# Block 1 of a mixer kernel computes two gates with eight plain products, and the weight sums for the later blocks move there

## The reference

```python
h = rms_norm(x, norm_g[l]) * (1.0 + scale[:, None, :]) + shift[:, None, :]
proj = h @ w_in[l]
...
o_gate = jax.nn.sigmoid(proj[..., OFF_O:OFF_ZM])
z_mlstm = proj[..., OFF_ZM:OFF_G]
...
hm = mlstm_chunkwise(q, k, v, ig, lf)
...
mlstm_out = hm.astype(x.dtype) * o_gate * jax.nn.silu(z_mlstm)
```

## Time and profile before

| | before |
|---|---|
| median of three runs | 1773.0 us |
| the profiled execution | 1772.9 us |
| its span, first to last instruction | 1771.1 us |
| PE busy | 1720.6 us, 97% |
| DVE, ACT, POOL busy | 1261.6, 709.6, 310.4 us |
| mean granted TensorE clock | 0.990 |
| DMA | 387.75 MB, mean 219 GB/s |

### The profile page before, as it was taken

How to read it: one execution, slowest core, us unless ns; L and a number is a source line. 1 busy time by engine, 2 the same in 40 slices (tenths; PEclk the granted TensorE clock), 3 DMA queues, 4 the chain that set the end, 5 groups by cost and what they waited for, 6 DMA issues and landing times.

```text
span 1771.1 us, 25354 instructions
## 1 busy us (share of the span) xinstructions
PE 1720.6 (97%) x8921; PEld 1475.0 (83%) x8921; DVE 1261.6 (71%) x2599; ACT 709.6 (40%) x1636; POOL 310.4 (18%) x265
## 2 busy tenths in 40 slices
PE   5996999999999999999999999999999999999998
PEld 5885787988888888988889888888889888898886
DVE  7784687666876678766876668766787667876683
ACT  4443334343443535334343434345343353433421
POOL 0022113021130302103030121303022030300300
PEclk9998999999999999999999999999999999999999
DMA  9998884679646895569846797468955598466852
GB/s 334 337 319 336 247 247 108 229 218 288 171 156 212 231 297 139 191 191 250 277 104 220 209 277 199 122 237 238 289 140 192 189 259 266 117 216 199 253 167 83
DMA packets 393554, 387.75 MB, mean 219 GB/s; under 512 B 258300, under 2 KB 283860, under 8 KB 392916
## 3 DMA queue, kind: packets, MB, share of 16 engines
q1 hardware_dynamic: 378196, 363.44, 66.9%
q10 hardware_dynamic: 15232, 22.69, 4.2%
HBM read 323.99 MB, written 62.06 MB: 218 GB/s over the span
## 4 chain that ended last, share of the span: by engine, by line
PE 87%; DVE 5%; DMA 4%; issue 2%; ACT 1%; SPq 0%; POOL 0%; ACTq 0%; DVEq 0%; POOLq 0%
PE ps_acc L717 19%; PE ps_acc L719 19%; PE ps_acc L718 19%; PE ps_num L719 4%; PE ps_num L717 4%; PE ps_num L718 4%; PE ps_kv L717 2%; PE ps_kv L718 2%; PE ps_kv L719 2%; PE ps_sco L1007 2%; PE ps_num L1026 1%; PE ps_kv L1032 1%; PE ps_num L1025 1%; DMA s_kept<-sb_x_res 1%; DVE sb_ada_raw L1691 1%
## 5 line engine op out<-in xcount | busy, mean ns | idle before, releaser
L717 PE MATMUL ps_acc<-sb_hT_hi,sb_w_split 128*128 128x512 f32 x1024 | 406.8, 397 | 1.1 <-DVE sb_w_split L1839 1.0
L719 PE MATMUL ps_acc<-sb_hT_hi,sb_w_split 128*128 128x512 f32 x1024 | 400.0, 391 | 0.0
L718 PE MATMUL ps_acc<-sb_hT_lo,sb_w_split 128*128 128x512 f32 x1024 | 399.2, 390 | 0.0
L719 PEld LDWEIGHTS ps_acc<-sb_hT_hi,sb_w_split 128*128 128x128 f32 x1024 | 192.6, 188 | 41.4
L717 PEld LDWEIGHTS ps_acc<-sb_hT_hi,sb_w_split 128*128 128x128 f32 x1024 | 192.9, 188 | 40.9 <-issue 1.9
L718 PEld LDWEIGHTS ps_acc<-sb_hT_lo,sb_w_split 128*128 128x128 f32 x1024 | 193.0, 188 | 37.7
L1544 POOL TENSOR_TENSOR sb_w_split<-sb_w_raw,sb_w_split 128x512 fp32r<-128x512 f32 x84 | 116.5, 1395 | 559.5 <-ACT sb_w_split L1108 559.4
L1108 ACT ACTIVATE sb_w_split<-sb_w_raw 128x512 fp32r<-128x512 f32 x140 | 85.9, 631 | 80.3 <-DMA sb_w_raw<-s_kept 76.5
L2067 DVE SCALAR_TENSOR_TENSOR sb_acc_cv<-sb_shifted,sb_par,sb_acc_cv 128x512 f32<-128x512 f32 x96 | 73.7, 767 | 60.7 <-ACT sb_acc_cv L1377 58.2
L1861 DVE TENSOR_TENSOR sb_w_split<-sb_w_raw,sb_w_split 128x512 fp32r<-128x512 f32 x56 | 56.9, 1017 | 69.3 <-ACT sb_w_split L1108 69.0
L1555 POOL TENSOR_TENSOR sb_h_rs<-sb_h_var,sb_mhalf 128x4 f32<-128x4 f32 x32 | 32.4, 1012 | 400.3 <-DVE sb_h_var L2161 400.3
(11 more groups left out here) (287 smaller groups left out, 3935.0 us busy)
## 6 DMA issues: line engine op xcount, KB each, us to landing
sb_w_split<-w_kept SPq DMA_DIRECT2D x288, 512.0 KB, 4.4
sb_w_split<-w_kept SPq DMA_DIRECT2D x56, 520.0 KB, 4.5
sb_w_raw<-s_kept SPq DMA_DIRECT2D x112, 256.0 KB, 4.3
sb_w_raw<-w_in SPq DMA_DIRECT2D x76, 256.0 KB, 4.6
sb_x_res<-x SPq DMA_DIRECT2D x34, 512.0 KB, 4.7
w_kept<-sb_w_split SPq DMA_DIRECT2D x32, 512.0 KB, 6.2
out<-sb_qT SPq DMA_DIRECT2D x32, 512.0 KB, 2.9
sb_x_in<-x SPq DMA_DIRECT2D x112, 128.0 KB, 3.9
```

The lines of the kernel that those rows point to most:

```text
L717: pe.matmul(dst, st_hi, mv_hi, start=start, stop=False, skip_group_check=resumed)
L718: pe.matmul(dst, st_hi, mv_lo, start=False, stop=False, skip_group_check=resumed)
L719: return pe.matmul(dst, st_lo, mv_hi, start=False, stop=stop, skip_group_check=resumed)
```

## The change

Block 1 does its z and o as block 0 does: eight plain products, two gates of eight k-steps in four chunks, in place of seven products. Each gate has four banks of its own there. Its zo stage has 16 units, eight from `w_kept` and eight raw (w_in's o columns; ACT splits them, POOL makes the low parts), so `UNITS` and `TILE_UNITS` have three kinds of blocks. The weight sums leave block 0. In block 1 they have four buffers, `s_raw`, over the memory of `mixm`, the row broadcasts, `fg`, `x_in` and `x_res`; SP loads them at units 26 to 29, DVE sums all four after `turn_keys`, SP stores them at units 35 to 38 and waits for the stores at unit 40, ahead of the next block's x; ACT waits for them ahead of its row broadcasts. `keep_keys` stands at units 33 to 40, two for each unit.

```diff
-SUM_TILES = {8 + 2 * r: r for r in range(4)}
-SUM_LOADS = {28: 0, 35: 1, 39: 2, 43: 3}
-SUM_STORES = {34 + 4 * r: r for r in range(4)}
+SUM_LOADS = {26: (0,), 27: (1,), 28: (2,), 29: (3,)}
+SUM_STORES = {35: 0, 36: 1, 37: 2, 38: 3}
+SUMS_KEPT = 40
...
+        s_raw = nc.alloc_sbuf_tensor_at("sb_s_raw", [P, 4, 2, D], F32, offset=sums_at)
-        zo_first = [acc[0], acc[1], bro, num[1]]
+        zo_first = [[[acc[0], acc[1], bro, num[1]]] * 2, [[acc[0], acc[1], sco, bro], [num[0], num[1], kv[0], kv[1]]]]
...
             def load_sums(r):
-                if r == 0:
-                    sp.wait_ge(x_T, PREPS)
-                else:
-                    sp.wait_ge(w_sum_kept, 16 * r)
+                sp.wait_ge(acc_full, TASKS)
+                sp.wait_ge(o_ready, NC)
+                sp.wait_ge(x_turned, NC)
...
# first_block, SP
-                    if m in SUM_STORES:
-                        keep_sums(SUM_STORES[m])
-                    if m in SUM_LOADS:
-                        load_sums(SUM_LOADS[m])
...
-                        sp.wait_ge(w_sum_kept, 64)
...
+            def second_block():
+                for m in range(LOW, UNITS[1]):
+                    if QK_END <= m < TILE_UNITS[1]:
+                        load_zo(1, m - QK_END)
+                    else:
+                        load_w(1, m)
+                    for r in SUM_LOADS.get(m, ()):
+                        load_sums(r)
+                    if m in SUM_STORES:
+                        keep_sums(SUM_STORES[m])
+                    if m == SUMS_KEPT:
+                        sp.wait_ge(w_sum_kept, 64)
+                    if m in (40, 42):
+                        load_x(2, (m - 40) // 2)
...
# zo_unit, PE
-                    w_wait(m)
+                    if first or n == 0:
+                        w_wait(m)
+                    else:
+                        pe.wait_ge(zo_lo_pool, k + 1)
...
# heads_to_scores, PE
-                        if not first:
-                            pe.wait_ge(zo_summed, 8 * b)
+                        if b >= 2:
+                            pe.wait_ge(zo_summed, 8 * (b - 1))
+                        elif b == 1:
+                            pe.wait_ge(zo_mixed, 8 * b + NC)
...
# ACT
+                def zo_second():
+                    exponents()
+                    for u in range(8, 12):
+                        split_zo(b, u)
+                    act.wait_ge(rows_kept_done, 32 * (b + 1))
+                    for u in range(12, 14):
+                        split_zo(b, u)
+                    zo_gates(0)
+                    act.wait_ge(w_sum_kept, 64)
+                    load_m_row(0)
+                    load_inter_row(0)
+                    for u in range(14, 16):
+                        split_zo(b, u)
+                    zo_gates(1)
...
# DVE
+                def zo_second():
+                    for h in range(NH):
+                        turn_keys(h)
+                    for r in range(4):
+                        sum_w(r)
+                    for n in range(2):
+                        zo_first_mixes(n)
...
-                    if first and t in SUM_TILES:
-                        sum_w(SUM_TILES[t])
```

More of the change, by code:

```diff
@@ L100, with kind @@
 OFFSET = {"q": OFF_Q, "k": OFF_K, "u": OFF_U, "zp": OFF_ZP}
[L103 to L110, removed]
+def kind(b):
+    return min(b, 2)
 def unit0(b, name, i):
     n = TILES.index((name, i))
-    return V_UNITS + 2 * n if n < 8 else TILE_UNITS[late(b)] + 2 * (n - 8)
+    return V_UNITS + 2 * n if n < 8 else TILE_UNITS[kind(b)] + 2 * (n - 8)
 def slot(b, m):
-    return m % RING if m < TILE_UNITS[late(b)] else (m + 2 * late(b)) % LOW
-SLOT_UNITS = [[[m for m in range(UNITS[b]) if slot(b, m) == s] for s in range(RING)] for b in range(2)]
+    return m % RING if m < TILE_UNITS[kind(b)] else (m + 2 * (kind(b) == 2)) % LOW
+SLOT_UNITS = [[[m for m in range(UNITS[b]) if slot(b, m) == s] for s in range(RING)] for b in range(3)]
 def before(b, m):
-    units = SLOT_UNITS[late(b)][slot(b, m)]
+    units = SLOT_UNITS[kind(b)][slot(b, m)]
     n = units.index(m)
@@ L132, in before @@
         return b, units[n - 1]
-    return (b - 1, SLOT_UNITS[late(b - 1)][slot(b, m)][-1]) if b and slot(b, m) < LOW else None
+    return (b - 1, SLOT_UNITS[kind(b - 1)][slot(b, m)][-1]) if b and slot(b, m) < LOW else None
 def loads(b, m):
@@ L139, in loads @@
     gates = 1
-    return gates + so_far([len(SLOT_UNITS[k][s]) for k in range(2)], b) + SLOT_UNITS[late(b)][s].index(m) + 1
+    return gates + sum(len(SLOT_UNITS[kind(a)][s]) for a in range(b)) + SLOT_UNITS[kind(b)][s].index(m) + 1
 U_UNITS = [unit0(0, "u", g) + half for g in range(4) for half in range(2)]
@@ L373, in unit_used @@
             else:
-                t, half = divmod(m - V_UNITS if m < QK_END else 16 + m - TILE_UNITS[late(b)], 2)
+                t, half = divmod(m - V_UNITS if m < QK_END else 16 + m - TILE_UNITS[kind(b)], 2)
                 if half == 0:
@@ L657, in late_block @@
                         load_w(b, m)
-                    if m == TILE_UNITS[1] and not last:
+                    if m == TILE_UNITS[2] and not last:
                         sp.wait_ge(zo_full, zo_no(b, 7, 1))
                         load_x(b + 1, 0)
-                    if m == TILE_UNITS[1] + 5 and not last:
+                    if m == TILE_UNITS[2] + 5 and not last:
                         load_x(b + 1, 1)
@@ L682, in one_block @@
                 if not last:
-                    order = (1, 2, 3, 4, 0) if first else range(LOW)
+                    order = (1, 2, 3, 4, 0) if b < 2 else range(LOW)
                     for n in range(4):
@@ L959, in zo_unit @@
                         last.then_inc(zo_used, 1)
-                for t in range(16 if first else 8):
+                for t in range(16 if b < 2 else 8):
                     if t < 8:
@@ L1413, in one_block @@
                             zo_gates((t - 8) // 4)
-                if not first:
+                if b == 1:
+                    zo_second()
+                elif b >= 2:
                     zo_late()
@@ L1574, in one_block @@
                 else:
-                    for u in ZO_POOL:
+                    for u in range(8, 16) if b == 1 else ZO_POOL:
                         low_zo(b, u)
```

138 lines of the change are left out of this document (83 added, 55 removed).

## The result

The changed kernel takes 1775.9 us (median of 20 runs, 1773.1 to 1779.8) where the kernel before takes 1772.3 (20 runs, 1768.8 to 1775.6): a ratio of 1.0022, with a 95% interval of 1.0015 to 1.0028. It is slower by about 3.6 us; 6.2 less was forecast, and 1775.9 lies outside the range of 1762.0 to 1772.6. The profiled execution took 1774.5 us (span 1772.7), 1.6 more than the one before.

The account below looks back on a forecast made before the run. PE, busy 97% of the span, bounds the kernel with its work plus its waits in block 0. A 3.4 + B 3.2 + C 5.0 - price 5.4 = 6.2 us less: 1766.7 from 1772.9; 8-in-10 range 1762 to 1772.6.

Parts of the forecast that it names:

- The price in block 1: Block 1's z and o stage: 24 more matmuls at 0.2267 us cost 5.4 us, all on PE.
- rival 3: Block 1: ACT's wait for the stored sums becomes PE's wait, making the kernel slower, 1778 us; chance 0.10.
- Loads of the next block's x ... Nothing: Block 1: x loads move to units 40 and 42, issued at about Z + 30, and cost nothing.
- Z: Start of block 1's new z and o stage, from which the forecast counts its times in us.
- A: Block 0, PE's 3.42 us wait before 149.14, through ACT's wait for fold stores: gain 3.4 us, between 0 and 4.1.
- B: Block 0, PE's 9.62 us wait before 161.10, for the first mix of z: gain 3.2 us, 6.4 of idle stay.
- Rival 2: Part of block 0's gain is given back: A stays, C's clock is waited out at D, or both; about 1770.5; chance 0.23.
- C: Block 0, PE's 3.94 us wait before the first scores at 195.69: 2.5 of idle and 2.5 of clock, gain 5.0 us.
- D: I leave it: PE's two waits of 1.9 us each at block 0's end, taken as unchanged; between -2.5 and 3.8 us.
- C's clock is waited out at D: Second part of Rival 2: C's clock gain of 2.5 us is lost in the waits at block 0's end; 1769 us.

Follow-up runs that it names:

- e12_scores_24: e1_x2_later with 24 added 128x128 matmuls on PE between wait C and block 0's first scores; by the medians the time grows by 1.8 us.
- e1_x2_later: Changed kernel with the next block's x loaded in block 1 behind weight units 46 and 48 instead of 40 and 42; 1772.6 us.
- e2_no_sums: Kernel before, seven products in block 1, with the weight sums left out everywhere (later products use wrong weights); 1767.7 us.
- e6_four_folds: e1_x2_later with four buffers instead of two for the folds' outputs; 1769.7 us.
- e11_keep_order: e6_four_folds with block 0's first turned heads kept behind units 51 and 55 and the residual behind 51, x left behind 43; 1768.6 us, ratio 0.9976.

## Why the prediction was wrong

- **The price in block 1: right.** 0.2267 us a matmul and 5.44 us for the 5.4 forecast, in every trace but that of e12_scores_24 with its slower clock. No wait inside the stage, and the fourth store of the sums was no trouble (rival 3): the four landed within 5.7 us, SP went on at 398.63. DVE's sums were late by five overlaps with POOL, as many as rival 3 counted; that went into SP's lead.
- **"Loads of the next block's x ... Nothing": this step failed.** It looked at when x would be issued (Z + 29 before, Z + 32 measured) and not at what stands behind it on SP. In the changed kernel weights that PE needs within 12 us of the first scores stand behind eight slow DMAs; in the kernel before only four of them stood there, as the second half of x came five units behind the first and not two. It cost 3.2 us by the medians (e1_x2_later), 4.3 in the traces, half of it clock. The forecast set SP's waits at units 35 to 38 against a lead of 17 us and then took nothing off this lead for the x loads.
- **A: right in what it waits for, mis-sized in the gain.** 3.4 was forecast, as the stores were to land earlier without 2 MB beside them. The landing that A waits for took 13.6 us before and 12.2 after, and still 13.2 in e2_no_sums. From the first fold product to B's end the changed trace gains 5.2 us (37.10 to 31.86), of which 3.0 are B's; the other traces with two buffers have gains of 3.0 to 4.7 there, so A gave 0 to 2.2. e6_four_folds shows that this landing is A. Rival 2 had this as its first part. That the longest landing hardly changed fits the rule on the sharing of the DMA engines (the Trainium skill, "DMA: Bandwidth & Descriptors", Queues, rings and completion order); no run tests the rule by itself.
- **B: right.** Idle 6.61 us for the 6.4 that were to stay, at half clock afterwards.
- **C: right at its place, but worth at most about one of its five us; "D: I leave it" is the second step that failed.** The idle fell to 1.68 (1.5 forecast), the clock stayed up, 4.8 us in all. But the end of block 0 followed the last fold product by some 84 us with C's loss and without it, which the added matmuls confirm for 4 of 5.4 us. The forecast priced C on PE's timeline alone; beside it unit 46 waits behind the x loads, and DVE goes on 20.1 us behind the last fold product for 20.4. The rival had "C's clock is waited out at D", 2.5 us, and needed nearly the whole of C.
- **The sum.** By the traces: folds -6.0, C -2.3, the stretch to the x sums +1.6, the price +5.4, block 1's heads +4.4, the rest -0.6 and the start -1.0, together +1.6 for the profiled pair. Against the forecast of -6.2 and the medians' +3.6, A is short by some 2, C by some 4, and unit 43 takes 3 to 4.

## What to carry to other kernels

A gain at a wait counts only if the next wait on the same engine isn't fed by a chain that runs beside it: measure, in the trace before, the distance from the event that starts that chain (here the last fold product, for which SP waits) to the later wait, and ask whether the wait that goes lies inside it. On a queue that issues in order, a step that is moved is priced by what stands behind it and by the lead that is left there, and a lead is spent once: here the sums took 6.7 us of it and the x loads the rest.

## What the runs showed of the hardware

- Three of the four DMAs of x at 398.63 took SP 0.7 to 0.8 us to issue, one held it for 6.2 (400.12 to 406.30); the DMA share is 1.05 from 390 to 400 and 0.92 from 400 to 410. Later in the block, from 475.44 on, each of four such DMAs takes 0.6 to 0.7, at a share of 0.46. So the issue of one kind of DMA cost SP up to ten times as much at a share of 0.9 and more; that it waits for room in the queues is a reading that no run tests.
- The granted clock after a wait of 2 to 3 us isn't settled by its length. After the wait for `sb_silu_zp` it stayed at 1.00 in one trace (2.81 us of idle, e6_four_folds, the first row) and was at 0.50 in another (2.67, e11_keep_order, the second); after 1.7 us at C it was at 1.00 in every trace, after 3.94 at half:

```profile
253.84:256.00 2.16, 2.16 (x9) 1.00 0.17 27
```

```profile
252.46:255.00 2.54, 2.54 (x6) 0.50 0.36 65
```
